# A gather by matrix products in a mixture-of-experts block: three bf16 parts, or fp32 rows scaled once, with the first tile's gather moved ahead

## What is computed

```python
# x: (256, 1024), after mixer and cross-attention
hf = rms_norm(x, norm_ffn_g)
logits = hf @ router_w + router_b            # 32 experts
top_logits, top_idx = lax.top_k(logits, 4)
gates = softmax(top_logits)
# for each expert e: its tokens' rows
gu = x_rows @ w_gate_up[e] + b_gate_up[e]    # (1024, 2048)
act = (clip(up) + 1) * min(gate, 7) * sigmoid(1.702 * gate)
y_rows = act @ w_down[e] + b_down[e]         # (1024, 1024)
y = scatter-add of y_rows * gate             # then x + y, and the last norm
```

## Time and profile before

| what | value |
|---|---|
| median of 3 runs | 1185.32 us (1185.07 to 1187.43) |
| the profiled execution's own time | 1184.91 us |
| its span in the trace | 1183.2 us |
| TensorE busy | 1104.2 us, 93% |
| weight loads on TensorE | 533.5 us, 45% |
| VectorE busy | 350.3 us, 30% |
| ScalarE busy | 167.0 us, 14% |
| bytes moved | 435.65 MB, mean 368 GB/s |

### The profile page before, as it was taken

One profiled execution on the slowest core, in us unless ns is written; L12 is line 12 of the kernel. 1 busy time (PEld: TensorE's weight loads), 2 busy tenths in 40 slices (PEclk: granted clock), 3 DMA queues, 4 the chain that ended last, 5 costly groups with the idle time before them and its releaser, 6 DMA issues.

```text
span 1183.2 us, 13909 instructions
## 1 busy us (share of the span) xinstructions
PE 1104.2 (93%) x5819; PEld 533.5 (45%) x5819; DVE 350.3 (30%) x741; ACT 167.0 (14%) x272; POOL 4.0 (0%) x23
## 2 busy tenths in 40 slices
PE   7999999999999999999898989898989898989897
PEld 5889886764334333433333333333334333333332
DVE  4685244454213212212121212122212212121213
ACT  3431233441101000000000010101010101010002
POOL 1000000000000000000000000000000000000000
PEclk9999999999999999999999999999989999999999
DMA  9832324667999999999999999999999999999996
GB/s 341 301 128 86 128 86 116 245 279 314 430 426 429 427 427 436 425 431 429 431 427 432 430 433 429 432 429 432 429 430 433 428 433 429 432 427 433 424 426 245
DMA packets 39605, 435.65 MB, mean 368 GB/s; under 512 B 5877, under 2 KB 5962, under 8 KB 20394
## 3 DMA queue, kind: packets, MB, share of 16 engines
q1 hardware_dynamic: 37642, 433.67, 87.3%
q10 hardware_dynamic: 1920, 1.34, 0.6%
HBM read 433.95 MB, written 1.05 MB: 368 GB/s over the span
## 4 chain that ended last, share of the span: by engine, by line
PE 62%; DMA 35%; DVE 1%; ACT 1%; issue 1%; SPq 0%; DVEq 0%; PEldq 0%
DMA ring<-in_w_down 34%; PE ps L2016 17%; PE ps L2061 17%; PE ps L1577 4%; PE ps L1688 4%; PE ps L2076 3%; PE ps L1634 3%; PE ps L1684 2%; PE ps L1557 2%; PE ps L1745 2%; PE ps L1985 2%; PE ps L1821 1%; PE ps L1865 1%; DMA ring<-in_w_in 1%; PE ps L2004 1%
## 5 line engine op out<-in xcount | busy, mean ns | idle before, releaser
L2061 PE MATMUL ps<-ring,work 128*64 128x512 f32 x1024 | 244.2, 626 | 40.9 <-DMA ring<-in_w_down 38.2
L2016 PE MATMUL ps<-ring,work 128*64 128x512 f32 x1024 | 225.6, 593 | 8.5 <-DMA ring<-in_w_gate_up 8.5
L2016 PE MATMUL ps<-work 128*64 128x512 f32 x1024 | 230.5, 592 | 0.0
L2061 PEld LDWEIGHTS ps<-ring,work 128*64 128x64 f32 x1024 | 80.1, 143 | 180.2 <-issue 162.9
L2016 PEld LDWEIGHTS ps<-ring,work 128*64 128x64 f32 x1024 | 71.4, 137 | 158.3 <-issue 141.2
L2016 PEld LDWEIGHTS ps<-work 128*64 128x64 f32 x1024 | 71.7, 137 | 136.3 <-issue 129.1
L1429 DVE TENSOR_SCALAR work<-ps 128x512 f32<-128x512 f32 x32 | 21.9, 686 | 197.1 <-PE ps L1557 197.1
L1452 DVE COPY work<-ps 128x512 f32<-128x512 f32 x16 | 11.1, 691 | 223.4 <-PE ps L1557 223.4
L1464 DVE COPY work<-ps 128x512 f32<-128x512 f32 (+1 forms) x16 | 11.1, 691 | 221.5 <-PE ps L2061 221.5
L2076 PE MATMUL ps<-work 128*128 128x512 f32 (+1 forms) x132 | 59.7, 608 | 10.4 <-ACT work L800 10.1
L1557 PEld LDWEIGHTS ps<-small,work 128*128 128x128 f32 (+1 forms) x354 | 44.9, 170 | 51.2 <-issue 45.1
(11 more groups left out here) (241 smaller groups left out, 728.3 us busy)
## 6 DMA issues: line engine op xcount, KB each, us to landing
work<-in_w_gate_up SPq DMA_DIRECT2D x64, 2048.0 KB, 36.6
ring<-in_w_gate_up SPq DMA_DIRECT2D x22, 4096.0 KB, 32.2
ring<-in_w_down SPq DMA_DIRECT2D x22, 4096.0 KB, 36.1
ring<-in_w_gate_up SPq DMA_DIRECT2D x20, 2048.0 KB, 21.6
ring<-in_w_down SPq DMA_DIRECT2D x17, 2048.0 KB, 20.4
ring<-in_w_in SPq DMA_DIRECT2D x7, 2048.0 KB, 15.5
ring<-in_xattn_w_kv SPq DMA_DIRECT2D x2, 2048.0 KB, 14.4
ring<-in_w_out SPq DMA_DIRECT2D x2, 2048.0 KB, 8.2
```

Source lines behind the costliest of these rows:

```text
L2016: last = nc.tensor.matmul(bank(b)[p], xg_T[k][:, kb, :], quad_columns(w[:, kk, D_MODEL * (q // 2):D_MODEL * (q // 2 + 1)], q % 2), start=F ...
L2061: last = nc.tensor.matmul(bank(Y_BANK + y)[p], act_T[k][:, b, HALF * c:HALF * c + HALF], w[:, b, 512 * q:512 * q + 512], start=False, stop ...
```

## The change

Each row is scaled by rstd once on ScalarE into an fp32 matrix scaled_rows, and the gather is made of fp32 products of it with an fp32 pick: 8 blocks x 2 tiles = 16 products for an expert or, in gather_both, for two. Parts, remainders and the turns of keep_turning are gone; picks move to another place and are fp32. The first tile's slots product stands before the last logits of the second tile; VectorE places the first tile's slots and picks for expert 0 ahead of `choose_experts(1)`, and TensorE gathers the first tile (`gather_first(0)`) ahead of the remaining slots products. The second tile's part (`gather_first(1)`) completes it.

```diff
-        split = [as_bf16(at, TILES * D_MODEL).rearrange("p (a b) -> p a b", b=D_MODEL)
-                 for at in (M2, M2 + 1024, QKT)]
-        remainder = [area(HT + 1024, D_MODEL), area(HT, D_MODEL)]
+        scaled_rows = area(M2, TILES, D_MODEL)
+        square_parts = area(HT + 1024, D_MODEL)
...
-        picks = as_bf16(HT + 1920, TILES * 2 * SLOTS).rearrange("p (a b) -> p a b", b=2 * SLOTS)
+        picks = area(QKT, TILES, 2 * SLOTS)
...
-            def split_high(t):
+            def scale_rows(t):
                 act.wait_ge(S("x2_inverse"), t + 1)
                 for h in range(2):
-                    nc.scalar.activation(split[0][:, t, half_cols(h)], half_of(t, h), ACT.Copy,
-                                         scale=by_tile(rstd, t)).then_inc(S("split_high"), 1)
-
-            def split_mid(t):
...
+                    nc.scalar.activation(scaled_rows[:, t, half_cols(h)], half_of(t, h), ACT.Copy,
+                                         scale=by_tile(rstd, t)).then_inc(S("rows_scaled"), 1)
...
+            v.wait_ge(S("first_slots_filled"), 1)
+            place_slots(0)
+            pick_tile(0, 0, 0).then_inc(S("first_tile_picked"), 1)
             choose_experts(1)
-            split_rest(1, 0)
-
             filled(v, "slots")
...
+            place_slots(1)
...
-                    pick_one(0, 0).then_inc(S("picked_first"), 1)
-                    split_rest(1, 1)
-                    split_low(1, 0)
-                    split_low(1, 1)
+                    pick_tile(0, 0, 1).then_inc(S("picked_first"), 1)
                     pick_one(1, 0).then_inc(S("picked"), 1)
                     count_tokens()
...
+            pe.wait_ge(S("before_ready"), 2)
+            pe.wait_ge(S("chosen_ready"), 1)
+            take(pe, "slots")
+            mm(pair("slots")[:, 0:E], before, chosen_b[:, 0, :]).then_inc(S("first_slots_filled"), 1)
             router_logits(1, 4, 6, 3)
             router_logits(1, 6, KB, 0)
...
-            keep_turning(12)
-            pe.wait_ge(S("before_ready"), 2)
...
+            def gather_first(t):
+                for b, columns in enumerate(block_columns):
+                    if b in (0, 2):
+                        pe.wait_ge(S("rows_scaled"), TILES * t + 1 + b // 2)
+                    last = nc.tensor.matmul(bank(GATHER_BANK[0])[:, SLOTS * b:SLOTS * b + SLOTS],
+                                            scaled_rows[:, t, columns], pick[0][:, t, :],
+                                            start=(t == 0 and b == 0), stop=(t == TILES - 1 and b == KB - 1))
+                return last
...
+            def gather_both():
+
+                for b, columns in enumerate(block_columns):
+                    for t in range(TILES):
+                        last = nc.tensor.matmul(bank(GATHER_BANK[b // 4])[:, P * (b % 4):P * (b % 4) + P],
+                                                scaled_rows[:, t, columns], picks[:, t, :],
+                                                start=(t == 0), stop=(t == TILES - 1))
...
+            pe.wait_ge(S("first_tile_picked"), 1)
+            gather_first(0)
             pe.wait_ge(S("chosen_ready"), TILES)
...
-            keep_turning(18)
```

More of the change, by code:

```diff
@@ L1342, in _, with place_slots, pick_tile @@
             x2_inverse(1)
+            def place_slots(t):
+                nc.vector.scalar_tensor_tensor(slot_m[:, t, :], pair("slots")[:, t * E:t * E + E], 1.0,
+                                               chosen_b[:, t, :], ALU.add, ALU.mult).then_inc(S("slots_placed"), 1)
+                v.wait_ge(S("slots_placed"), t + 1)
+            def pick_tile(k, i, t):
+                return nc.vector.tensor_scalar(pick[k][:, t, :], iota_s, slot_m[:, t, bass.ds(2 * i + k, 1)],
+                                               None, ALU.is_equal)
+            v.wait_ge(S("first_slots_filled"), 1)
+            place_slots(0)
+            pick_tile(0, 0, 0).then_inc(S("first_tile_picked"), 1)
             choose_experts(1)
[L1344 removed]
             filled(v, "slots")
[L1347 to L1350 removed]
+            place_slots(1)
             def gate_values():
@@ L1942, in _ @@
-            pe.wait_ge(S("before_ready"), 2)
+            block_columns = [slice(j, 256, 2) for j in range(2)] + [slice(256 + j, 768, 4) for j in range(4)] \
+                + [slice(768 + j, 1024, 2) for j in range(2)]
+            def gather_first(t):
[6 more added lines that the diff above has]
+                return last
@@ new lines, in gather @@
+            def gather(k):
+                for b, columns in enumerate(block_columns):
+                    for t in range(TILES):
+                        last = nc.tensor.matmul(bank(GATHER_BANK[k])[:, SLOTS * b:SLOTS * b + SLOTS],
+                                                scaled_rows[:, t, columns], pick[k][:, t, :],
+                                                start=(t == 0), stop=(t == TILES - 1))
+                last.then_inc(S("gather_filled"), 1)
+            def gather_both():
+                for b, columns in enumerate(block_columns):
+                    for t in range(TILES):
+                        last = nc.tensor.matmul(bank(GATHER_BANK[b // 4])[:, P * (b % 4):P * (b % 4) + P],
+                                                scaled_rows[:, t, columns], picks[:, t, :],
+                                                start=(t == 0), stop=(t == TILES - 1))
+                    if b % 4 == 3:
+                        last.then_inc(S("gather_filled"), 1)
@@ L1943, in _ @@
+            pe.wait_ge(S("first_tile_picked"), 1)
+            gather_first(0)
             pe.wait_ge(S("chosen_ready"), TILES)
-            take(pe, "slots")
-            mm(pair("slots")[:, 0:E], before, chosen_b[:, 0, :])
             nc.tensor.matmul(pair("slots")[:, E:2 * E], ones, chosen_b[:, 0, :], start=True, stop=False)
@@ L2131, in begin_pass @@
                 pe.wait_ge(S("picked_first"), PAIRS * r + 1)
-                gather(0, opening)
+                if opening:
+                    gather_first(1).then_inc(S("gather_filled"), 1)
+                else:
+                    gather(0)
             def second_gather(r):
```

66 lines of the change are left out of this document (5 added, 61 removed).

## The result

The changed kernel took 1197.62 us (median of 4 runs, 1195.75 to 1198.48) beside 1185.32 us for the kernel before (median of 3): ratio 1.010, 95% interval 1.0086 to 1.0114. It is slower by 12 us, where 2.7 us were forecast. The profiled execution took 1195.75 us, 10.8 more than the one of before.

A forecast was written before the change was run, and what follows sets the result against it. The weight stream was taken to set the pace, anchored by the second chunk's release. Opening -0.6, second gather +2.2 and tail +1.1 gave +2.7 us on 1185.3, so 1188.0; range 1185.0 to 1191.5.

The forecast's parts named there:

- The bound and the anchor: Whole kernel: the weight stream sets the pace, its start anchored by the second chunk's release; longer gathers covered in the pairs.
- The order's gain: Opening: first tile gathered ahead of the remaining slots products, so VectorE's scaling starts earlier; gain 0.6 us, bounds 0.2 and 0.9.
- The price of a strided record: Gathers: a 16-byte step costs up to 0.04 us more a record, taken as 0.012; 16 products take 3.8 us.
- the rival at 7 in 100: Gathers: strided fp32 weights read at half the pace, records at 0.224, a gather 5.4; sum +7.7, 1193.0; 7 in 100.
- The granted clock: Opening: clock held at 1.00; rival that it falls without the turns, 2 to 3 us more, 1190.5; 6 in 100.
- forecast: +1.6: Opening: the longer second gather (+2.2) less the earlier opening (0.6) makes the stream 1.6 us later.
- Tail (+1.1): After the last DMA piece: the fp32 gather of both experts, 3.8 for 2.68, is uncovered; +1.1 us, 0.8 to 1.5.

The follow-up runs named there:

- rows block by block, with turns: Changed kernel with scaled rows stored block by block (weights read with step one), plus two turns and eight turns in the opening: 1186.63 us, ratio 1.0019.
- the changed kernel with turns: Changed kernel, strided as it is, plus two turns ahead of the first tile's gather and eight behind the slots' products: 1195.93 us, ratio 1.0098.
- old order: Changed kernel, strided fp32 products kept, with the order and the 12 and 18 turns of the kernel before: 1200.3 us, ratio 1.0126.
- the version block by block without turns: Changed kernel with scaled rows stored block by block, so that gather weights are read with step one; no turns: 1189.81 us, ratio 1.0048.
- the one that gathers both experts: Changed kernel with rows stored block by block and the opening's gather made for both experts at once, no second gather: 1185.14 us, ratio 1.000.
- parts ahead: Kernel before, bf16 parts kept, first tile gathered ahead of the second choice for both experts at once, no second gather, 12 turns: 1188.32 us, ratio 1.0032.

## Why the prediction was wrong, by its steps

**The bound and the anchor: right.** Doubling the gathers cost no 40 us, and the later pairs kept their waits for w_down, 12 of them, up to 2.6 us (3.16 before). Take as the stream's start the point at which the second load begins to flow less 4.88 us. Before it is 280.55 + 1.7 - 4.88 = 277.37, after 288.76 + 1.7 - 4.88 = 285.58. To the start of the last pair's last down (1111.43 and 1119.36) it is then 834.06 and 833.78 us: the pairs together have one length, though TensorE does 2.9 us more in each.

**The order's gain (-0.6): right in mechanism.** With no step and the clock held (rows block by block, with turns) the first release came 10.19 us after the logits, 1.07 earlier than before. The second gather then cost 3.79 - 1.60 = +2.2, as forecast.

**The price of a strided record (0.012, at most 0.04 us dearer): this step failed.** It is 0.116 dearer, 0.233 for 0.117. I took it from turns at the same step, and read only their own time, 0.15 us more over four. Their weight loads (PEld) were in the same trace. Four turns of slices with step one, then the four of up_sb:

```profile
287.30 0.42 PEld L1557 LDWEIGHTS ps<-small,work 128*128 128x128 f32 x4 [0.81 <-issue]
302.20 0.56 PEld L1557 LDWEIGHTS ps<-small,work 128*128 128x128 f32 x4 [0.81 <-issue]
```

The loads grew by a third, so the step did cost something there; but it is not the doubling either. Why a strided turn shows so little of what a strided gather pays no run shows, and so the turns were no bound for another kind of product. This was the rival at 7 in 100, and its 0.224 was near; I held the turns against it. The Trainium skill, page "SBUF — State Buffer", "Specifications (TRN2)", says that a line has 16 bytes and wants two hits for full bandwidth. The trace of the gathers agrees: twice the time at a step of 16 bytes (0.233), hardly more at 8 (0.117) than at step one (3.57/32 = 0.112). Opening, from the two kernels with turns: 2 x 1.02 for the tiles and 5.83 - 3.79 = 2.04 for the second gather, **4.1 us**; tail 5.61 - 3.57 = **2.0 us**.

**The granted clock, held at 1.00 in the sum and its fall put at 6 in 100: failed too.** The second release moved by +10.06. Of it +1.04 is the kernel block by block with turns (forecast: +1.6); +5.78 is what the changed kernel with turns adds, 4.1 of step and 1.7 of the fall at 280.40; the last +3.24 is the first fall, which the turns took away. So the clock cost **4.9 us** in the profiled execution. The second fall's 1.7 fits its length: 3.41 us of full work at half the clock lose 1.7. The first fall's 3.24 rests on two profiles; the medians of these two kernels lie only 1.7 apart, as by their mean clocks the executions with turns differ in their falls. I had argued that the idle pieces are short, 0.5 us behind the logits and 1.1 behind the slots. They were shorter still, 0.04 and 0.75, and the clock fell, so the argument looked for the cause in idle alone. Two changes were shown to bring a fall, each with the other left out: idle where the turns stood (the kernel before with its turns moved), and strided fp32 gathers with the turns in place (old order).

**Tail (+1.1): right in mechanism**, +2.9: 3.57 - 2.68 = 0.9 without the step, and 2.0 for the step.

**Sum:** the forecast 2.7, less 0.6 for an opening that was better than forecast (1.04 for 1.6), less 0.2 in the tail, plus 4.1 and 2.0 for the step, plus 4.9 for the clock: 12.9. The medians say 12.3 (1197.62 less 1185.32). In the profiled execution the logits came 1.85 earlier: 11.1, against 10.8 measured.

**What stays open.** Which trait of a strided fp32 gather lowers the clock, or rather goes with its fall. In the steady pairs the gather of both experts is as strided (5.61 us at a clock of 1.00), and the falls of before behind the waits for w_down are nearly gone, one at 1109.12; in the opening the second gather, 64 columns a product, has a fall within 1.4 us of its end in each of the four profiles of strided versions that have one, and the strided gather of both experts there, 128 columns, has one too. Why the version block by block without turns fell at 263.90 already, with only some 0.3 us of idle ahead of it, isn't settled either; the one that gathers both experts had 0.28, 0.20 and 0.97 us of waits there, no turns and no fall.

## What to carry to other kernels

A saving in the number of products is worth nothing while the transfers pace. But what stands between the first two releases of a buffer is paid in full once they are further apart than one chunk's transfer, since it delays the whole stream. When a matrix product's stationary operand goes from bf16 to fp32, look at its step in bytes, not in elements, and price it by a stream of products of that step, not by a few turns. A change that takes turns or idle work away has to be costed with the clock at its lower level as a likely case.

## What the runs showed of the hardware that I had not expected

**Weights at a step of 16 bytes take twice the time**, 0.233 us a record for 0.117; at 8 bytes little is lost (0.117 for 0.112), and storing the rows in blocks costs ScalarE's copies nothing that shows in the opening's times. This pace did not change with the clock. In the changed kernel's second tile, at a granted clock of 0.50, seven strided records take from 268.58 to 270.22, 0.234 us each (the windows' counts again take in neighbours):

```profile
268.58:270.22 1.64, 1.64 (x9) 1.64 (x9) 0.50 0.06 25
```

Records of step one went from 0.112 to 0.21 there (the version block by block without turns, 268.62 to 270.33).

**Stalls at the loop, with packets of the instruction queue.** Three programs made from the kernel before with another number of instructions of TensorE (gathers twice, no turns, parts ahead) stalled at the first products of a pair, twice, 175 to 178 us apart, which is the length of the loop of three pairs. These are the waits of TensorE from 640 to 850 us in the kernel with bf16 parts in the new order, and the instruction queue's packets in the same stretch:

```profile
PE ps L2033 <- issue: 12.4, 2, 6.3
```

```profile
q8 instruction: 12, 0.20, 0.4%
```

The same stretch of the kernel before has no such wait, and in that queue:

```profile
q8 instruction: 1, 0.02, 0.0%
```

In the kernels with gathers twice and without turns that queue has 14 and 12 packets there, in the ten other profiles 1. So loop instructions that are loaded again are the likely cause, but no run varied that alone. With the 30 turns moved and not removed the stalls were gone. The number of instructions by itself does not decide it: the nine profiles of fp32 versions, with several counts, have no stall. The stalls go with 3.5 to 4.5 us more of stream, though the DMA share stayed at 9 tenths or more. An experiment that changes the instruction count ahead of a loop can bring this cost with it; the packets of the instruction queue tell.

**A full DMA share does not mean that TensorE's lateness is free**: the stream's length, counted as above, grew from 834.1 us to 837.5 (no turns), 838.1 (parts ahead) and 838.6 (gathers twice). In the other profiles it is 833.8 to 835.7. The growth is 0.4 to 0.5%, too little for a share in tenths to show.
